# Where the expert stage keeps its weights and its own data: fifteen weight places and a dozen buffers change their addresses

## The reference

```
x = x + gate_m * hybrid_mixer(h, ...)            # two attentions, then merged @ w_out
h = rms_norm_2(x, g_ffn_norm) * (1 + scale_f) + shift_f
x = x + gate_f * moe_ffn(h, ...)
return rms_norm_2(x, g_final)

def moe_ffn(h, ...):
    scores = sigmoid(h @ w_router)               # 64 experts, 4 of 8 groups, 6 experts a token
    routed = sum over the chosen experts e of gate_e * (silu(h @ w_exp_gate[e]) * (h @ w_exp_up[e])) @ w_exp_down[e]
    shared = (silu(h @ w_sh_gate) * (h @ w_sh_up)) @ w_sh_down
    return shared + routed
```

## Time and profile before

| | |
|---|---|
| median of 3 runs | 1056.14 us (1056.07 to 1057.98) |
| profiled execution | 1059.31 us, its span 1057.3 us |
| TensorE busy | 1018.6 us, 96% of the span |
| VectorE, ScalarE, GpSimd busy | 562.4, 396.1, 380.5 us |
| HBM read | 318.72 MB |
| granted TensorE clock, mean | 0.987 |

### The profile page before, as it was taken

One profiled execution on the slowest core, in us unless ns is written; L12 is line 12 of the kernel. 1 busy time (PEld: TensorE's weight loads), 2 busy tenths in 40 slices (PEclk: granted clock), 3 DMA queues, 4 the chain that ended last, 5 costly groups with the idle time before them and its releaser, 6 DMA issues. The chain is left out here.

```text
span 1057.3 us, 14798 instructions
## 1 busy us (share of the span) xinstructions
PE 1018.6 (96%) x5952; PEld 741.1 (70%) x5952; DVE 562.4 (53%) x1022; ACT 396.1 (37%) x680; POOL 380.5 (36%) x309
## 2 busy tenths in 40 slices
PE   8999998999999899999999999999999999999997
PEld 7878886888887687888777565565656565555653
DVE  5899789867766785766667221222222222222243
ACT  5646765556334553657344111121212111111213
POOL 1399999992994069698000000000000000000000
PEclk9999999999999999999999999999999999999999
DMA  9966766477585476555289999999999999999994
GB/s 322 315 220 223 236 219 219 139 244 264 185 254 192 151 250 236 162 174 173 91 255 416 359 415 416 416 416 415 417 416 414 416 415 415 416 417 417 415 416 184
DMA packets 92469, 320.75 MB, mean 303 GB/s; under 512 B 8785, under 2 KB 11889, under 8 KB 75761
## 3 DMA queue, kind: packets, MB, share of 16 engines
q1 hardware_dynamic: 84448, 290.90, 72.1%
q0 software_dynamic: 7664, 28.37, 8.3%
q10 hardware_dynamic: 288, 0.52, 0.1%
HBM read 318.72 MB, written 1.05 MB: 302 GB/s over the span
## 5 line engine op out<-in xcount | busy, mean ns | idle before, releaser
L875 PE MATMUL ps<-hl,L 128*128 128x512 f32 (+1 forms) x1216 | 385.5, 399 | 10.3 <-DVE L L1765 5.6
L875 PEld LDWEIGHTS ps<-hl,L 128*128 128x128 f32 x1216 | 229.1, 192 | 61.0 <-issue 14.6
L1765 DVE TENSOR_TENSOR rlo<-ring,hl 128x1024 fp32r<-128x1024 f32 (+1 forms) x154 | 212.3, 1395 | 79.7 <-ACT hl L1338 79.0
L875 PE MATMUL ps<-rlo,L 128*128 128x512 f32 (+1 forms) x608 | 239.3, 394 | 0.0
L875 PE MATMUL ps<-slots_all,xe 128*64 128x256 f32 x2048 | 230.2, 381 | 1.1 <-DVE rt L2569 1.1
L1338 ACT ACTIVATE hl<-ring 128x1024 fp32r<-128x1024 f32 (+1 forms) x154 | 160.6, 1054 | 129.5 <-PE ps L875 118.4
L875 PEld LDWEIGHTS ps<-slots_all,xe 128*64 128x64 f32 x2048 | 144.8, 137 | 77.1 <-issue 5.1
L864 POOL CAST two<-ident 64x128 fp32r<-64x128 f32 x64 | 18.9, 295 | 480.7 <-PE ps L875 479.3
L818 POOL TENSOR_SCALAR mring<-mring,st 128x512 f32<-128x512 f32 x84 | 173.9, 2071 | 2.0 <-DMA mring<-in_w_mod 0.4
L875 PEld LDWEIGHTS ps<-rlo,L 128*128 128x128 f32 x608 | 116.1, 191 | 24.6
L820 POOL TENSOR_TENSOR macc<-macc,mring 128x512 f32<-128x512 f32 x84 | 121.9, 1452 | 7.0
(11 more groups left out here) (234 smaller groups left out, 915.3 us busy)
## 6 DMA issues: line engine op xcount, KB each, us to landing
slots_all<-in_w_exp_gate SPq DMA_DIRECT2D x64, 1024.0 KB, 22.4
slots_all<-in_w_exp_up SPq DMA_DIRECT2D x64, 1024.0 KB, 22.2
slots_all<-in_w_exp_down SPq DMA_DIRECT2D x62, 1024.0 KB, 22.7
ring<-in_w_in SPq DMA_DIRECT2D x48, 1024.0 KB, 5.5
mring<-in_w_mod POOLq DMA_DIRECT2D x48, 512.0 KB, 4.3
ring<-in_w_out SPq DMA_DIRECT2D x8, 1024.0 KB, 5.2
ring<-in_w_ple_gate SPq DMA_DIRECT2D x4, 1024.0 KB, 6.1
ring<-in_w_branch_a SPq DMA_DIRECT2D x4, 1024.0 KB, 5.5
```

Source lines behind the costliest of these rows:

```text
L875: return e.matmul(o, l, r, start=start, stop=stop)
L1765: return e.tensor_tensor(o, a, b, op)
```

## The change

The fifteen first places of the stream are new: entries 0 to 5 go over `bs` and the attention's last buffers (X1 + 24, 0, 40, 32, 60 and 68 KB), entry 6 over `mring`, 7 and 10 to 13 over `ring`, 8 and 9 over L1, and 14 at X1 + 8 KB. They are issued earlier: entry 0 behind the first ring load of `of0`, entries 1 and 2 behind that of `wp0`, 3 to 5 behind that of `wp1` (`early`), the others behind the last ring load. The stage's own data move over `hl` (HL) and L0 (XL), `ht3` to X1 + 16 KB. The two loads of `shb`, now in L0, are issued behind entry 13 and a wait for the end of the dense stage. `hi_of` shifts its turn of the places, and VectorE waits for one more piece before it writes `xp`, which now lies over `hl`. The number of places, the entries and their order are the same.

```diff
-        ht3 = place("ht3", [128, 8, 256], at=X1)
-        h3hl = place("h3hl", [128, 2, 2, 1024], F32R, at=X1 + 8 * K)
-        xe = place("xe", [128, 8, 512], at=X1 + 24 * K)
+        MR, HL, XL = X0 + 40 * K, X0 + 48 * K, X0 + 72 * K
+        ht3 = place("ht3", [128, 8, 256], at=X1 + 16 * K)
+        h3hl = place("h3hl", [128, 2, 2, 1024], F32R, at=HL)
+        xe = place("xe", [128, 8, 512], at=XL)
...
-        xp = place("xp", [128, 2, 1024], at=X1 + 16 * K)
-        shb = place("shb", [128, 8, 320], at=X1 + 24 * K)
+        xp = place("xp", [128, 2, 1024], at=HL + 16 * K)
+        shb = place("shb", [128, 8, 320], at=XL)
...
-            return hl[:, g % NH, 0:2 * pieces[g][2]].rearrange("p (k n) -> p k n", k=2)
-        place2 = [5] + [(len(loads) + q) % NS for q in range(NS)] + [11, 12, 6, 7, 8, 9, *range(13, NE), 10]
+            return hl[:, (g - npieces + 4) % NH, 0:2 * pieces[g][2]].rearrange("p (k n) -> p k n", k=2)
+        last_ring = range(nloads - NS, nloads)
+        in_ring = [X0 + 8192 * (i % NS) for i in last_ring]
+        place_at = [X1 + 24 * K, X1, X1 + 40 * K, X1 + 32 * K, X1 + 60 * K, X1 + 68 * K, MR, in_ring[0],
+                    X1 - 16 * K, X1 - 8 * K, *in_ring[1:], X1 + 8 * K]
+        first_of = {name: pieces[blocks[name][0]][0] for name in ("of0", "wp0", "wp1")}
+        early = {first_of["of0"]: (0,), first_of["wp0"]: (1, 2), first_of["wp1"]: (3, 4, 5)}
...
+            def emptied(i):
+                if i >= NE:
...
+                elif i == 0:
+                    w.wait_ge(pe_aux.sem, pe_aux.at[("km", 1, 4)])
+                elif i in (1, 2):
+                    w.wait_ge(pe_aux.sem, pe_aux.at[("s2", 7, 1)])
+                elif i == 3:
+                    w.wait_ge(pe_aux.sem, pe_aux.at[("o2", 7)])
+                elif i in (4, 5):
+                    w.wait_ge(pe_aux.sem, pe_aux.at[("omT", 1, 0)])
+                elif i == 6:
+                    w.wait_ge(mac, quarter_done(nq - 1))
+                elif i in (8, 9):
+                    w.wait_ge(pe_w, both(blocks["om1"][-1]))
+                elif i == NE - 1:
+                    w.wait_ge(sq2_a, 4)
+                else:
+                    freed(last_ring[0 if i == 7 else i - 9])
...
-            w.wait_ge(pe_aux.sem, pe_aux.at[("km", 1, 4)])
+                for q in early.get(i, ()):
+                    load_expert(q)
+            for i in range(6, NE - 1):
+                load_expert(i)
+            w.wait_ge(pe_w, 2 * npieces)
             e.dma_start(shb[:, :, 0:64], WSG[:, :, 192:256]).then_inc(shared_in, 16)
             e.dma_start(shb[:, :, 64:320], WSU).then_inc(shared_in, 16)
...
+            for i in range(NE - 1, len(loads2)):
+                load_expert(i)
...
                 wait_mine()
+                w.wait_ge(pe_w, both(npieces - 5))
                 tsc(xp[:, m, :], R[:, m, :], st[:, 70 + m:71 + m], None, ALU.mult, None).then_inc(xp_set, 1)
```

More of the change, by code:

```diff
@@ L147, in two_blocks @@
         assert X0 + 13 * 8192 <= X1
-        ht3 = place("ht3", [128, 8, 256], at=X1)
-        h3hl = place("h3hl", [128, 2, 2, 1024], F32R, at=X1 + 8 * K)
-        xe = place("xe", [128, 8, 512], at=X1 + 24 * K)
-        yy = place("yy", [128, 2, 1024], F32R, at=X1 + 40 * K)
-        sh_ = place("sh_", [128, 2, 768], at=X1 + 40 * K)
+        MR, HL, XL = X0 + 40 * K, X0 + 48 * K, X0 + 72 * K
+        ht3 = place("ht3", [128, 8, 256], at=X1 + 16 * K)
+        h3hl = place("h3hl", [128, 2, 2, 1024], F32R, at=HL)
+        xe = place("xe", [128, 8, 512], at=XL)
+        yy = place("yy", [128, 2, 1024], F32R, at=HL + 16 * K)
+        sh_ = place("sh_", [128, 2, 768], at=HL + 16 * K)
         hh = place("hh", [128, 3, 256], at=X1 + 48 * K)
@@ L160, in two_blocks @@
         slots_all = place("slots_all", [128, (X1 + 60 * K + (NE - 13) * 8192) // 4], at=0)
-        place_at = [X0 // 4 + 2048 * j for j in range(13)] + \
-                   [(X1 + 60 * K) // 4 + 2048 * j for j in range(NE - 13)]
         assert base + X1 + 60 * K + (NE - 13) * 8192 <= nc.sbuf_usable_end
@@ L165, in two_blocks @@
         assert base + X1 + 62 * K + (NE - 13) * 8192 <= nc.sbuf_usable_end
[L166 to L170, removed]
-        xp = place("xp", [128, 2, 1024], at=X1 + 16 * K)
-        shb = place("shb", [128, 8, 320], at=X1 + 24 * K)
-        fb = place("fb", [128, 2, 1024], at=X1 + 24 * K)
-        bt = place("bt", [128, 2, 512], at=X1 + 20 * K)
-        junk = place("junk", [128, 2, 1024], at=X1 + 32 * K)
+        gfin = place("gfin", [128, 1024], at=HL)
+        yz = place("yz", [128, 2, 1024], F32R, at=HL + 4 * K)
+        yz_plain = place("yz_plain", [128, 2, 1024], at=HL + 4 * K)
+        yy_plain = place("yy_plain", [128, 2, 1024], at=HL + 16 * K)
+        hb = place("hb", [128, 256], at=HL + 12 * K)
+        xp = place("xp", [128, 2, 1024], at=HL + 16 * K)
+        shb = place("shb", [128, 8, 320], at=XL)
+        fb = place("fb", [128, 2, 1024], at=XL)
+        bt = place("bt", [128, 2, 512], at=HL + 12 * K)
+        junk = place("junk", [128, 2, 1024], at=XL + 8 * K)
         PS = [ctx.enter_context(nc.psum_tensor(f"ps{i}", [128, 512], F32)) for i in range(8)]
@@ L321, in hi_of @@
         def hi_of(g):
-            return hl[:, g % NH, 0:2 * pieces[g][2]].rearrange("p (k n) -> p k n", k=2)
-        place2 = [5] + [(len(loads) + q) % NS for q in range(NS)] + [11, 12, 6, 7, 8, 9, *range(13, NE), 10]
+            return hl[:, (g - npieces + 4) % NH, 0:2 * pieces[g][2]].rearrange("p (k n) -> p k n", k=2)
[3 more added lines that the diff above has]
+                    X1 - 16 * K, X1 - 8 * K, *in_ring[1:], X1 + 8 * K]
+        assert len(place_at) == NE
+        first_of = {name: pieces[blocks[name][0]][0] for name in ("of0", "wp0", "wp1")}
+        early = {first_of["of0"]: (0,), first_of["wp0"]: (1, 2), first_of["wp1"]: (3, 4, 5)}
         loads2, at2 = [], {}
@@ L355, in slot2 @@
         def slot2(name):
-            a = place_at[place2[at2[name] % NE]]
+            a = place_at[at2[name] % NE] // 4
             return slots_all[:, a:a + 2048]
@@ L722, in load_beside, with load_expert @@
                     e.dma_start(wkv_up[:, :], D["w_kv_up_2"]).then_inc(up_in, 16)
+            def emptied(i):
+                if i >= NE:
+                    name = loads2_of[i - NE]
+                    if name == "shared":
+                        w.wait_ge(pe_aux.sem, pe_aux.at["router"])
+                    elif name == "sd":
+                        w.wait_ge(sh_pe, 1)
+                    elif name[0] == "d":
+                        w.wait_ge(pe_aux.sem, pe_aux.at[("d", name[1] // 2, 1)])
+                    elif name[0] == "g":
+                        w.wait_ge(pe_aux.sem, pe_aux.at[("gate", name[1] // 2)])
+                    else:
+                        w.wait_ge(pe_aux.sem, pe_aux.at[("gu", name[1] // 2)])
+                elif i == 0:
[12 more added lines that the diff above has]
+                    w.wait_ge(sq2_a, 4)
+                else:
+                    freed(last_ring[0 if i == 7 else i - 9])
+            def load_expert(i):
+                k, src = loads2[i]
+                name = loads2_of[i]
+                emptied(i)
+                dst = slot2(name)[:, 0:k * src.shape[2]].rearrange("p (a b) -> p a b", a=k)
+                if name[0] == "d" and name[1] >= 62:
+                    dst = slot2(name).rearrange("p (a b) -> p a b", a=2)[:, :, 0:512]
+                if name == "shared":
+                    dst = slot2("shared").rearrange("p (a b) -> p a b", a=8)
+                    e.dma_start(dst[:, :, 0:64], WR).then_inc(shared_in, 16)
+                    dst = dst[:, :, 64:256]
+                e.dma_start(dst, src).then_inc(slot2_sem[i % NE], 16)
             for i, (kind, parts) in enumerate(loads):
```

## The result

| | before | after |
|---|---|---|
| median | 1056.38 us (1056.07 to 1057.98, 4 runs) | 1067.24 us (1065.9 to 1068.94, 4 runs) |
| ratio | | 1.0095, 95% interval 1.0081 to 1.0108 |
| span of the profiled execution | 1057.3 us | 1066.1 us |

The account below looks back on a forecast made before the run. The expert stage was taken as bound by the weight stream, TensorE close behind. Early loads 0, stall 6.6 and clock 2.4 us summed to 9.0, on 1056.1: 1065.1 us forecast, 8-in-10 range 1061.0 to 1067.0.

Parts of the forecast that it names:

- Part 1: First places moved and loads 0 to 6 issued earlier, beside the ring loads: gain 0, cost 0, 1 us at most.
- entry 16 hangs on its place: Expert weight stream: 471.2 us from entry 16's issue to the end hang on TensorE's time, not on early entries.
- Part 2: Router product on TensorE waits for the moved `shb` loads, since `shared_in` at 48 counts them: stall of 6.6 us.
- the landing of entry 13: Load ahead of `shb` in the queue: issued at 555.73, lands 5.2 us later at 560.9.
- the 3.1 us of `shb` up behind its gate part: Queue behind entry 13: `shb` up lands 3.1 us after the gate part, at 565.1 us.
- Part 3: TensorE behind the stall, up to the router product's end: half-rate clock costs 2.4 us, from 0 to 3.1.
- The sum: All ahead of entry 16's issue: 0 + 6.6 + 2.4 = 9.0 us, giving 1065.1 us and a span of 1066.3.
- behind entry 16 nothing absorbs the delay: Expert stream after entry 16's issue: each load waits for a place returned 9.0 us later; the 471.2 us stay.
- The stall alone: Rival at the router product: clock stays at 2.4 GHz, 1062.7 us; chance 0.15, shared with a smaller stall.
- The head start that reaches the end: Rival in the expert stream: early entries remove 11.4 us of waiting, 1044.7 us, or 1053.7 with a stall; chance 0.04.
- No effect on the path: Rival at the router product: `shb` lands before it is needed or the wait is met otherwise, 1056.1 us; chance 0.06.

Follow-up runs that it names:

- e1: Changed kernel with the `shb` loads on their own semaphore, so the router product waits for the router columns alone; ratio to the kernel before 1.0002.
- e7: e1 without the early entries: entries 0 to 13 go out behind the last ring load, in the new places; ratio to the kernel before 1.0089.
- e9: e7 with `shb` issued at the dense stage's end, ahead of entries 5 to 14; ratio to the kernel before 1.0013.
- e2: Kernel before with only the two `shb` loads moved, behind entry 5 and a wait for the dense stage's end; ratio to the kernel before 1.0084.
- e3: Changed kernel with 34 extra products on TensorE between the first turn and the router product; ratio to the kernel before 1.0070.
- e5: Changed kernel with the two `shb` loads issued ahead of entry 13 instead of behind it; ratio to the kernel before 1.0081.

## Why the prediction was right

**Part 1, cost and gain 0.** Right: e1 holds all of part 1 and stands at 1.0002. The reason given, that entry 16 hangs on its place, is shown by B (471.3 before, 471.2 in e1 with the head start) and by the steps of B with the number of places. What I missed is the second office of the early entries, that they keep the queue in front of `shb` short (e7), and that first loads late enough to keep the queue running at entry 16 do cost something (1.5 us of B in e9).

**Part 2, the stall, 6.6 us.** The mechanism was right, e1 and e2 take it away and bring it about alone. The size: the wait before the router product grew from 1.69 to 9.29 us, and 0.25 us of a later wait fell away, so 7.35 us. The term that was off is the landing of entry 13, 6.0 us after its issue instead of the 5.2 read from the same load before; the 3.1 us of `shb` up behind its gate part I had nearly right (564.64 - 561.65 = 3.0).

**Part 3, the clock, 2.4 us.** From the router product to the product with `shb` it is 12.39 us after and 568.39 - 558.28 - 0.25 = 9.86 before: 2.5 us. e3 takes 2.5 us off A by keeping TensorE at work. Its own stretch is 9.63 us, so against e3 the clock costs 2.8 us and the stall 7.1; the difference is that the later wait in the kernel before costs 0.48 us (10.11 - 9.63) and not only the 0.25 that its row prints. The sum is the same.

**The sum.** 7.35 + 2.5 = 9.9 us in A, 0.0 in B, against 9.0. The medians differ by 10.9 and the ratio says 8.6 to 11.4. The predicted span was 1066.3, the measured 1066.1, which flatters: the dense stage happened to end 1.15 us early in that profile. That behind entry 16 nothing absorbs the delay was right to 0.1 us in this profile; in e2, e3 and e5, with a stall of the same kind, B is 0.3 to 0.9 us shorter than before.

**The rivals.** The stall alone (no clock) is 2.5 us short. The head start that reaches the end: none of it in e1. No effect on the path: the wait is on it.

## What to carry to other kernels

When a load moves, look up every wait that counts its semaphore, not only the instruction that reads the data: here the first reader had 3 us to spare, and a product that shared the counter paid 7.4. And ask of a stream through a ring of places what starts it running without pause. If it is the return of a place, earlier first loads gain nothing once the queue is dry at that moment, and the lever that these runs show is another place. An earlier return should be one too; no run here tries it.

An empty stretch of DMA time next to a full ring is a place to put something: a store that frees SBUF for one more place cost nothing in A or B there.

## What I had not expected

The last load of a queue pays for all that was issued late in front of it: the same `shb` load took 8.2 us to land before, 9.1 in the changed kernel and 18.5 in e7. The megabyte of entry 16, behind a dry queue, took 4.8 to 4.9 us in the seven kernels with 15 places other than e9, and 8.1 us in e9 with the queue still running.

Two idle times of TensorE of 9.29 and 7.74 us were both followed by half rate, but the work at half rate behind them was of different length, so that shortening the stall by 1.5 us gave 2.5. The runs don't show what sets that length.
